# A second mixer on four parts of 128 tokens instead of two halves of 256, with its side tiles kept in SBUF and a router of one-hot products

## The chip, the cores and the metric

One core of a Trainium2 chip runs the whole program in one launch. The metric is the device time of one execution in microseconds (us). Before the change three runs took 3859.07, 3864.57 and 3869.43 us; the median is 3864.57 us. The trace is of one further execution, which took 3868.05 us.

## The reference, cut to what matters

512 tokens of 1024 columns, all in float32, go through two blocks. The first block (a mixer and product-key experts, where each token picks 128 rows out of two tables of 16384 rows) ends in a norm; the second block has two mixers side by side and 32 experts.

```python
x = x + gate1 * mix                                   # first block
h = rmsnorm(x, norm2_w[l]) * (1.0 + scale2) + shift2
x = x + gate2 * peer(h, ...)                          # per token: 128 rows of u, 128 rows of v
...
u, v = expert_u[idx], expert_v[idx]
act = gelu(einsum('td,thkd->thk', xb, u))             # "dots"
return einsum('thk,thkd->td', gate * act, v)          # "sums"
...
p = rmsnorm_2(x, attn_norm_g) @ w_in                  # second block: 10528 columns
y_a = rwkv7_mix(p[rwkv])      # a recurrence over the tokens, here in chunks of 64
y_b = ssd_mix(p[z, xbc, dt])  # a convolution of 4 taps, a recurrence in chunks of 128, gated by silu(z)
x = x + (g_a * (y_a @ w_up_rwkv) + g_b * (y_b @ w_up_ssd)) @ w_out
x = x + hier_moe(h)           # top group, top 2 of its 8 experts; 1024 assignments
out = rmsnorm(x, final_norm_g)
```

Both recurrences and the convolution run forward over the tokens, so a later part of the tokens needs only a small state of the earlier one. Every token meets all the weights of the second block: w_in with 43 MB, the three matrices behind it with 17 MB.

## The kernel before

Activations lie transposed in SBUF, features on partitions and tokens along the row (`xT`, `hT`: 8 tiles of 128 x 512). The mixers work on halves of 256 tokens (`Half`, L54). Weights come from HBM through four slots in `m.weights`, each a load of 1 MB (8 x 128 rows x 256 columns, rows of 1 KB); `project` (L284) fills a slot when its tiles have been multiplied, and `prefetch` (L272) fills all four ahead of time.

The work of `Peer` (L1211) is the product-key experts. GpSimd gathers 128 rows of 4 KB at a time (0.5 MB, L1268) into a ring of 12 slots; a "step" uses one slot: a dot (L1343) or a weighted sum (L1349) on VectorE, or, for the sums of tokens 0 to 127, a diagonal matrix made on VectorE (L1337) and two products on TensorE (L1361). There are 128 steps for each of four tiles of 128 tokens and each of two tables, 1024 in all. `sequence` (L1236) fixes their order. The steps stand in VectorE's queue in between the work of the mixers: after each piece of mixer work `beside(m, dve, us)` tells how long the engine would otherwise be free, and `go` (L1314) puts one step for each `pace` (1.8, 1.1 or 1.45) of it. The order is thus fixed when the program is built, and the engines wait for one another by semaphores alone. Each block of work ends in `meet`, where four engines wait for one another.

The stages, in order:

1. The first block's mixer, query projection and picking for tokens 0 to 255.
2. The same for tokens 256 to 511, with steps in between. The picks of this half are made at the end (`key_scores`), while TensorE does the diagonal sums of tile 0.
3. `peer.finish(1)` (L1377): the steps left of tiles 0 and 1, and nothing else. The sums of tile 1 are 128 steps in a row.
4. `after_first` and `second_mixer` for tokens 0 to 255, with the 512 steps of tiles 2 and 3 in between; `peer.finish(2)` ends them.
5. `after_first` and `second_mixer` for tokens 256 to 511, with nothing beside it.
6. `second_experts`: a norm, the rows turned back, `route`, `slot_columns`, 16 pairs of experts (L2775, 12 MB of weights each, in a ring of four buffers of 4 MB), `combine`.

`second_mixer` itself is: a norm; `project` of 26 tiles of w_in (r, k, v and the small ranks; ScalarE shifts each tile, L1995 to L1997, and VectorE keeps it, L2001); `rwkv` up to the chunks; `rwkv_chunks` (L1796) with one turn for each 64 tokens; the rest of `rwkv`; `ssd`; a norm; `second_merge` with three projections of 8 tiles. The other 56 tiles of w_in (16 z, 24 x, 16 gates) are multiplied by `Spare` (L1464) inside `rwkv_chunks`, 14 to a turn, from four slots of 0.5 MB (rows of 512 bytes), in between the small products of the recurrence, so that TensorE has work while VectorE and ScalarE answer. Each such tile is taken out of its bank by ScalarE (L1550 to L1559), an x tile is convolved by VectorE (L1536, L1539), and all go to `projected` in HBM (L1280); `second_ssd` and `second_merge` load them back.

`route` computes the experts' choice by a chain of small VectorE operations. It then scatters token numbers to `slot_token` in HBM (L2496) by eight indirect DMAs; `slot_columns` (L2615) loads and turns that list, and the experts gather their rows of `h_kept` by it. On SP's queue `route` has the store of `h_kept`, four loads of 4 MB, and eight stores of zeros into `y_rows` (L2472), and its block ends only when these have landed.

## Time and profile before

| | |
|---|---|
| median of 3 runs | 3864.57 us (3859.07 to 3869.43) |
| the profiled execution | 3868.05 us; span 3866.0 us, mean granted clock 0.829 |
| TensorE (PE), its weight loads (PEld) | 2701.5 us (70%), 1970.6 us (51%) |
| VectorE (DVE) | 2223.4 us (58%) |
| ScalarE (ACT), GpSimd (POOL) | 537.4 us (14%), 1331.2 us (34%) |
| DMA | 1006.32 MB, mean 260 GB/s; gathers 549.54 MB, 38.6% of 16 engines' span; loads of SP 406.66 MB, 29.2% |

The profile's slices show the stages. In the slices 10 to 23 of 40 (about 970 to 2320 us) the DMA row has 8 or 9 tenths; in the slices 24 to 32 (about 2320 to 3190 us) it has 1 to 4 tenths, and the PE row 5 to 9; in the slices 34 to 38 it has 9 tenths at 428 GB/s. The chain of waits that the page gives covers only the last stage here, so the stages are read from the windows view: for each stretch it has the busy time of each engine with its instructions, the granted clock, the busy share of the 16 DMA engines and the rate. GpSimd's busy time there is the writing of the gathers' descriptors. An instruction for two operands in float32 shows as two MATMUL records.

### The profile page before, as it was taken

How to read it: one execution, taken by the hardware profiler on the slowest of the kernel's cores; microseconds unless marked ns; L12 is line 12 of the kernel's file. 1: busy time of each engine (PE TensorE's matmuls, PEld its weight loads, DVE VectorE, ACT ScalarE, POOL GpSimd, SP SyncE). 2: the span in 40 equal slices, each digit the busy share in tenths (PEclk: the TensorE clock that was granted, in tenths of full speed). 3: DMA queues.
4: the chain of work that ended last, by engine and by line, in shares of the span. 5: the costliest groups of instructions: out<-in, count | busy, mean ns of one | idle time of the engine just before them, and what ended most of it. 6: DMA issues, size and time to landing. Idle time of an engine off the chain costs nothing. (4 is left out here: it accounts for less than half of the span.)

```text
span 3866.0 us, 44669 instructions
## 1 busy us (share of the span) xinstructions
PE 2701.5 (70%) x17677; PEld 1970.6 (51%) x17677; DVE 2223.4 (58%) x4122; ACT 537.4 (14%) x1041; POOL 1331.2 (34%) x1088
## 2 busy tenths in 40 slices
PE   5877443767970175899965473879998777587774
PEld 4756442554420164778754452758887656322221
DVE  6543898887859878778888888252222633100001
ACT  1120002100000012222211100132222210000001
POOL 0000367675777666567655455000000000100000
PEclk7988776788985597989976786979999788799997
DMA  7611689897999997899988798413332233899996
GB/s 275 205 44 55 224 297 339 275 373 288 360 350 372 361 342 261 277 339 362 368 303 272 238 356 292 136 43 95 98 102 64 77 131 110 335 427 428 428 428 283
DMA packets 446736, 1006.32 MB, mean 260 GB/s; under 512 B 30525, under 2 KB 292039, under 8 KB 431175
## 3 DMA queue, kind: packets, MB, share of 16 engines
q0 software_dynamic: 151200, 549.54, 38.6%
q1 hardware_dynamic: 262948, 406.66, 29.2%
q10 hardware_dynamic: 32387, 47.38, 3.4%
q8 instruction: 133, 2.18, 0.2%
q14 instruction: 68, 0.56, 0.0%
HBM read 972.01 MB, written 31.47 MB: 260 GB/s over the span
## 5 line engine op out<-in xcount | busy, mean ns | idle before, releaser
L1268 POOL DMA_INDIRECT ring<-in_peer_u_dram,index x512 | 696.8, 1361 | 760.9 <-POOLq L190 418.8
L1268 POOL DMA_INDIRECT ring<-in_peer_v_dram,index x512 | 597.6, 1167 | 337.7 <-DVE h_rows_b L1349 163.9
L334 PE MATMUL bank<-hT,weights 128*128 128x256 f32 x2240 | 513.2, 393 | 179.8 <-DMA weights<-in_w_in_dram 87.9
L334 PEld LDWEIGHTS bank<-hT,weights 128*128 128x128 f32 x2240 | 441.5, 198 | 250.9 <-issue 104.1
L1513 PE MATMUL bank<-hT,weights 128*128 128x256 f32 x1792 | 426.2, 393 | 53.7 <-DVEq L149 25.9
L1513 PEld LDWEIGHTS bank<-hT,weights 128*128 128x128 f32 x1792 | 340.3, 194 | 106.2 <-issue 55.4
L1349 DVE SCALAR_TENSOR_TENSOR h_rows_b<-ring,coef,h_rows_b 128x1024 f32<-128x1024 f32 x254 | 325.6, 1282 | 37.0 <-DMA ring<-in_peer_v_dram,index 9.9
L1343 DVE SCALAR_TENSOR_TENSOR ring<-ring,h_rows_a 128x1024 f32<-128x1024 f32 x256 | 304.8, 1220 | 62.9 <-DMA ring<-in_peer_u_dram,index 60.6
L1343 DVE SCALAR_TENSOR_TENSOR ring<-ring,h_rows_b 128x1024 f32<-128x1024 f32 x256 | 299.3, 1220 | 13.0 <-DMA ring<-in_peer_u_dram,index 7.7
L2480 POOL MEMSET weights<- 128x1024 f32 x1 | 1.0, 957 | 871.3 <-POOLq L160 871.3
L2696 PE MATMUL bank<-xp_ring,weights 128*64 128x512 f32 x1024 | 252.3, 650 | 67.2 <-DMA xp_ring<-in_w_exp_gate_dram 48.7
L1361 PE MATMUL bank<-ring,weights 128*128 128x512 f32 x512 | 225.6, 602 | 9.6 <-DVE weights L1337 9.5
L2696 PEld LDWEIGHTS bank<-xp_ring,weights 128*64 128x64 f32 x1024 | 80.3, 149 | 227.4 <-issue 184.5
L2756 DVE COPY weights<-bank 128x512 f32<-128x512 f32 x16 | 11.1, 692 | 310.9 <-PE bank L2708 310.9
L1349 DVE SCALAR_TENSOR_TENSOR h_rows_a<-ring,coef,h_rows_a 128x1024 f32<-128x1024 f32 x127 | 163.1, 1284 | 14.0 <-DVE h_rows_a L1349 1.0
L1361 PEld LDWEIGHTS bank<-ring,weights 128*128 128x128 f32 x512 | 98.5, 194 | 136.0 <-issue 136.0
L2800 POOL DMA_INDIRECT weights<-h_kept,mo_columns x16 | 15.1, 941 | 384.3 <-PE bank L2682 365.6
L2721 PE MATMUL bank<-xp_ring,weights 128*64 128x512 f32 x512 | 115.0, 601 | 23.8 <-DMA xp_ring<-in_w_exp_down_dram 23.1
L1854 DVE TENSOR_TENSOR rc_Y<-rc_Y,bank 128x512 f32<-128x512 f32 x40 | 27.3, 683 | 181.2 <-PE bank L1822 181.2
L334 PE MATMUL bank<-ssd_y,weights 128*128 128x256 f32 x512 | 116.6, 392 | 19.7 <-DVEq L149 8.9
L977 PE MATMUL bank<-ident,h_rows_a 128*128 128x128 f32 x16 | 3.7, 424 | 181.1 <-ACTq L142 181.1
L334 PEld LDWEIGHTS bank<-ssd_y,weights 128*128 128x128 f32 x512 | 100.6, 197 | 36.4 <-issue 21.9
(513 smaller groups left out, 3959.8 us busy)
## 6 DMA issues: line engine op xcount, KB each, us to landing
xp_ring<-in_w_exp_gate_dram SPq DMA_DIRECT2D x16, 4096.0 KB, 35.7
xp_ring<-in_w_exp_up_dram SPq DMA_DIRECT2D x16, 4096.0 KB, 33.4
xp_ring<-in_w_exp_down_dram SPq DMA_DIRECT2D x16, 4096.0 KB, 34.4
weights<-in_w_in_dram SPq DMA_DIRECT2D x112, 512.0 KB, 4.0
weights<-in_w_in_dram SPq DMA_DIRECT2D x54, 1024.0 KB, 10.8
weights<-in_w_out_dram SPq DMA_DIRECT2D x16, 1024.0 KB, 13.1
weights<-in_peer_w_query_dram SPq DMA_DIRECT2D x16, 1024.0 KB, 7.9
weights<-in_w_up_ssd_dram SPq DMA_DIRECT2D x16, 1024.0 KB, 11.7
```

The lines of the kernel that those rows point to most:

```text
L334: ins = pe.matmul(m.ps[b][:, 0:TH], m.weights[:, s, k, c * P:(c + 1) * P], rhs(k), start=(k == 0), stop=(k == k_tiles - 1))
L977: ins = pe.transpose(m.ps[k][:, t * P:(t + 1) * P], src[:, t, k * P:(k + 1) * P], m.ident[:, :])
L1268: pool.indirect_dma_start(out=self.ring[:, n % RING, :], out_offset=None, in_=self.tables[table], in_offset=bass.IndirectOffsetOnAxis(ap=s ...
L1343: dve.scalar_tensor_tensor(out=slot, in0=slot, scalar=1.0, in1=row, op0=ALU.mult, op1=ALU.mult, accum_out=dots[:, j:j + 1]).then_inc(self. ...
L1349: dve.scalar_tensor_tensor(out=row, in0=slot, scalar=coef[:, j:j + 1], in1=row, op0=ALU.mult, op1=ALU.add).then_inc(self.free, 1)
L1361: ins = pe.matmul(bank[:, :], self.diag[:, j % self.DIAGS, :], self.ring[:, n % RING, h * 512:(h + 1) * 512], start=(j == 0), stop=(j == P ...
L1513: ins = pe.matmul(self.m.ps[3 + q % 2][:, 0:TH], self.weights[:, (q + 2) % self.SLOTS, k, :], self.half.h[:, k, :], start=(k == 0), stop=( ...
L1854: dve.tensor_tensor(dst[:, :, :], dst[:, :, :], bank3(5 + j), ALU.add).then_inc(xy_kept, 1)
L2696: ins = pe.matmul(m.ps[2 + j][q, :], self.xT[:, k, q], self.ring[:, slots[j], h, k * DE:(k + 1) * DE], start=(k == 0), stop=(k == KT - 1))
L2721: ins = pe.matmul(m.ps[5 + b][q, :], self.hidT[:, k, q], self.ring[:, slot, h, k * D + b * 512:k * D + b * 512 + 512], start=(k == 0), sto ...
L2756: dve.tensor_copy(self.hidT[:, :, :].rearrange("p k r -> p (k r)"), self.m.ps[4][:, :]).then_inc(self.h_kept, 1)
L2800: pool.indirect_dma_start(out=x.xr[:, p % 2, :], out_offset=None, in_=x.h_rows, in_offset=bass.IndirectOffsetOnAxis(ap=columns[:, p:p + 1] ...
```

## The change

Tokens are taken through the second mixer in four parts of 128 (`Part`), each part begun once `peer.finish` has the sums of its own tile of rows. Tile 3 is the last of the steps' order, tile 2 now comes whole before it. The three first parts stand in the stretch with steps; the fourth comes behind it.

- `project`, `norm`, `group_norm` and `rwkv` work on 128 columns instead of 256, and `beside` in `project` is halved with them. `rwkv_chunks` has two turns in each part instead of four, with 28 side tiles in a turn instead of 14.
- The side tiles (z, x, gates) are written where they are used, in SBUF; nothing goes to `projected`. Their order is `xxzxxzxxzzgggg` twice, and there are four row buffers for the convolution instead of two.
- `ssd` runs once for each part. Its state goes to HBM at the end of a part (1 MB, on SP's queue) and comes back at the start of `ssd` of the next.
- Of `second_experts`, the rows are turned back inside `route`, behind the router's products, and kept by ScalarE; the eight stores of zeros now stand in `after_first` of the last part; the counts above 64, 128, ... are one comparison and one sum; the three counting products are over all tiles at once; `slot_token` is gone: for each of 8 columns of assignments VectorE writes a one-hot of the place in the slot (128 wide) and one of the block times the token (24 wide), and TensorE multiplies them into the list.
- `combine` takes the root and scales tile by tile.

```diff
+class Part:
+    def __init__(self, m, j):
+        self.j, self.first, self.last = j, j == 0, j == T // TQ - 1
+        tokens = slice(j * TQ, (j + 1) * TQ)
+        self.x, self.h = m.xT[:, :, tokens], m.hT[:, :, tokens]
+        self.room = m.halves[1 - j * TQ // TH].h
@@ project
-                beside(m, dve, 0.44 * k_tiles)
+                beside(m, dve, 0.44 * k_tiles * width / TH)
@@ Peer.sequence
         steps += second_dots[at:] + all_of(1, 1)
-        for table in range(2):
-            for tile in range(HT, TT):
-                steps += all_of(tile, table)
+        for tile in range(HT, TT):
+            steps += all_of(tile, 0) + all_of(tile, 1)
@@ Peer.finish
-        m, end = self.m, halves * self.HALF_STEPS
+        m, end = self.m, self.plan.index((tile, 1, PICKS - 1)) + 1
+        self.pace = LATE_PACE
@@ Spare
-    KINDS = "zxgxzxgxzxgxzg"
+    ROWS = 4
+    KINDS = "xxzxxzxxzzgggg" * 2
...
-        act.dma_start(self.dest[self.FIRST[kind] + n], y).then_inc(self.stored[q % self.SLOTS], 16)
@@ rwkv_chunks, TensorE
-                    i = spare.multiply(pe, i, 2 * KT)
+                    i = spare.multiply(pe, i, (4 * PER_STEP - 2) * KT)
...
-                        i = spare.multiply(pe, i, KT // 2 if l <= 2 else KT)
+                        i = spare.multiply(pe, i, PER_STEP * (KT // 2 if l <= 2 else KT))
@@ ssd
+            @block.sync
+            def _(sp):
+                if not part.first:
+                    sp.dma_start(state, carry.ssd).then_inc(carry.ssd_landed, 16)
@@ second_ssd
-                for j in range(SG):
-                    sp.dma_start(z[:, 4 * j:4 * j + 4, :],
-                                 projected[4 * j:4 * j + 4].rearrange("k p t -> p k t")).then_inc(z_landed[j], 16)
+            if not part.last:
+                sp.dma_start(carry.ssd, state).then_inc(carry.ssd_stored, 16)
             prefetch(m, sp, *then)
@@ route
-                        pool.indirect_dma_start(
-                            out=slot_token.rearrange("b (s a) -> (b s) a", a=1),
-                            out_offset=bass.IndirectOffsetOnAxis(ap=dest[:, n:n + 1], axis=0),
-                            in_=token[:, t:t + 1], in_offset=None).then_inc(scattered, 16)
+                for n in range(TT * TOP):
+                    dve.tensor_scalar(hot_slot[:, n, :], slots[:, :], placef[:, 0, n:n + 1], None,
+                                      ALU.is_equal).then_inc(spread, 1)
+                    dve.tensor_scalar(hot_block[:, n, :], blocks[:, :], placef[:, 1, n:n + 1],
+                                      token[:, n // TOP:n // TOP + 1], ALU.is_equal, ALU.mult).then_inc(spread, 1)
...
+                for n in range(TT * TOP):
+                    pe.wait_ge(spread, 2 * n + 2)
+                    ins = pe.matmul(m.ps[3][:, 0:BLOCKS], hot_slot[:, n, :], hot_block[:, n, :],
+                                    start=(n == 0), stop=(n == TT * TOP - 1))
@@ two_blocks
-                    peer.finish(1)
                     early.close()
-                    with stage(m):
-                        after_first(m, first, rows[0], cols1, at1, (w_in_2[0], R_TILES))
-                    rows_a.close()
-                    second_mixer(first, second, rk_masks, own, ssd_small)
-                    peer.finish(2)
+                    for part in m.parts[:-1]:
+                        peer.finish(part.j)
+                        with stage(m):
+                            after_first(m, part, rows[part.j // HT][:, part.j % HT:part.j % HT + 1], cols1, at1, (w_in_2[0], R_TILES))
+                        if part.j == HT - 1:
+                            rows_a.close()
+                        second_mixer(part, rk_masks, own, ssd_small)
+                    peer.finish(TT - 1)
                     m.stretch, m.side = None, None
```

Three places show what moves. The first is VectorE behind the picks. `ring` and `h_rows` are the gathered rows and the rows that they are dotted with or summed into; `weights<-ident,coef` is a diagonal; `xT<-bank,mod,xT` opens `after_first`. Before, the sums of tile 1 stand ahead of it:

```order
L1337 TENSOR_SCALAR weights<-ident,coef 128x128 x8
L147 UNCONDITIONAL_BRANCH
L1380 UNCONDITIONAL_BRANCH
L1333 TENSOR_TENSOR coef<-coef,gate 128x128
L1346 TENSOR_SCALAR h_rows_a<-ring,coef 128x1024
L1349 SCALAR_TENSOR_TENSOR h_rows_a<-ring,coef,h_rows_a 128x1024 x127
L147 UNCONDITIONAL_BRANCH
L1393 UNCONDITIONAL_BRANCH
L1371 COPY h_rows_a<-bank 128x512 x2
L147 UNCONDITIONAL_BRANCH
L980 UNCONDITIONAL_BRANCH
L985 SCALAR_TENSOR_TENSOR xT<-bank,mod,xT 128x256 x8
```

Now:

```order
L1356 TENSOR_SCALAR weights<-ident,coef 128x128 x8
L161 UNCONDITIONAL_BRANCH
L1411 UNCONDITIONAL_BRANCH
L1390 COPY h_rows_a<-bank 128x512 x2
L161 UNCONDITIONAL_BRANCH
L998 UNCONDITIONAL_BRANCH
L1003 SCALAR_TENSOR_TENSOR xT<-bank,mod,xT 128x128 x8
L1352 TENSOR_TENSOR coef<-coef,gate 128x128
L1365 TENSOR_SCALAR h_rows_a<-ring,coef 128x1024
L1368 SCALAR_TENSOR_TENSOR h_rows_a<-ring,coef,h_rows_a 128x1024 x2
```

The second mixer's work begins 128 steps earlier, and the sums of tile 1 stand within it.

The second place is VectorE inside a turn of `rwkv_chunks`, in the stretch with steps. `rc_Y` and `rc_X` (in `weights` now) are the matrices of the recurrence; `spare_leaving` and `x_tiles` are convolved side tiles. Before:

```order
L1854 TENSOR_TENSOR rc_Y<-rc_Y,bank 128x512
L1854 TENSOR_TENSOR rc_X<-rc_X,bank 128x512
L1536 TENSOR_SCALAR spare_leaving<-spare_rows,cols 128x256
L1539 SCALAR_TENSOR_TENSOR spare_leaving<-spare_rows,cols,spare_leaving 128x256 x3
L1343 SCALAR_TENSOR_TENSOR ring,dots<-ring,h_rows_b 128x1024 x8
```

Now:

```order
L1880 TENSOR_TENSOR weights<-weights,bank 128x512 x2
L1571 TENSOR_SCALAR x_tiles<-spare_rows,cols 128x128
L1574 SCALAR_TENSOR_TENSOR x_tiles<-spare_rows,cols,x_tiles 128x128 x3
L1571 TENSOR_SCALAR x_tiles<-spare_rows,cols 128x128
L1574 SCALAR_TENSOR_TENSOR x_tiles<-spare_rows,cols,x_tiles 128x128 x3
L1368 SCALAR_TENSOR_TENSOR h_rows_a<-ring,coef,h_rows_a 128x1024 x8
```

A level of the recurrence keeps its 8 steps and has two convolved tiles of half the width instead of one.

The third place is SP's queue over one part, the second of the four. It is the same for all parts but for the state, which the first does not load and the last does not store. `L286` is `prefetch`, with 16 loads of 1 MB behind the chunks; `L321` stands for the nine further loads of `project`; `L1543` are the 56 side tiles:

```order
L286 DMA weights<-in_w_in_dram 128x8x256 x4
...
L321 DMA weights<-in_w_in_dram 128x8x256
...
L1543 DMA weights<-in_w_in_dram 128x8x128 x2
...
L1543 DMA weights<-in_w_in_dram 128x8x128 x54
...
L1771 DMA rk_gates<-in_rwkv_w_g_dram 128x1024
...
L2125 DMA sd_state<-ssd_state 128x2048
...
L286 DMA weights<-in_w_up_rwkv_dram 128x8x256 x4
...
L2356 DMA ssd_state<-sd_state 128x2048
L286 DMA weights<-in_w_up_ssd_dram 128x8x256 x4
...
L286 DMA weights<-in_w_up_ssd_dram 128x8x256 x4
...
L286 DMA weights<-in_w_out_dram 128x8x256 x4
```

Before, the same loads of weights stand twice in the program, for 256 tokens each; now they stand four times.

## Rows read from the trace of the kernel before

**Rows 1.** Windows view: PE, PEld, DVE, ACT, POOL busy, granted clock, DMA share, GB/s.

```profile
1142.00:1319.00 177.00, 0.00 (x0) 0.00 (x0) 162.58 (x128) 0.00 (x0) 138.02 (x127) 0.50 0.98 369
1319.00:2411.00 1092.00, 766.35 (x6366) 626.61 (x6366) 893.71 (x1313) 194.14 (x412) 668.32 (x502) 0.81 0.89 312
```

**Rows 2.** Windows view, stages of the first 256 tokens, beside the expert rows.

```profile
1319.00:1364.00 45.00, 14.92 (x48) 11.90 (x48) 33.74 (x62) 7.24 (x19) 19.84 (x17) 0.65 0.86 300
1364.00:1482.00 118.00, 98.61 (x416) 83.75 (x416) 83.76 (x154) 18.70 (x78) 80.76 (x62) 0.93 0.98 357
1482.00:1557.00 75.00, 31.24 (x96) 18.49 (x96) 67.95 (x106) 22.47 (x35) 45.73 (x29) 0.57 0.65 210
1557.00:1991.00 434.00, 390.05 (x4760) 334.17 (x4760) 356.56 (x543) 107.41 (x211) 291.38 (x216) 0.93 0.95 337
1991.00:2255.00 264.00, 147.56 (x677) 105.90 (x678) 218.00 (x311) 38.31 (x69) 133.08 (x99) 0.68 0.79 269
2255.00:2359.00 104.00, 83.97 (x371) 72.41 (x369) 87.83 (x105) 0.00 (x0) 68.31 (x55) 0.92 0.98 357
```

**Rows 3.** Windows view, the same stages of the other 256 tokens, alone.

```profile
2421.00:2445.00 24.00, 11.24 (x32) 8.64 (x32) 10.54 (x20) 5.47 (x17) 0.00 (x0) 0.78 0.31 98
2445.00:2540.00 95.00, 92.95 (x416) 81.05 (x416) 13.07 (x28) 18.69 (x78) 0.00 (x0) 0.97 0.35 105
2540.00:2600.00 60.00, 38.84 (x130) 24.87 (x130) 38.63 (x53) 22.15 (x35) 0.00 (x0) 0.66 0.17 44
2600.00:2971.00 371.00, 363.50 (x4728) 312.11 (x4727) 102.37 (x176) 99.94 (x181) 0.00 (x0) 1.00 0.34 93
2971.00:3150.00 179.00, 130.26 (x726) 94.70 (x726) 99.85 (x214) 38.84 (x69) 0.00 (x0) 0.77 0.25 82
3150.00:3240.00 90.00, 85.63 (x384) 74.17 (x384) 19.90 (x49) 0.00 (x0) 0.00 (x0) 0.97 0.36 117
2421.00:3240.00 819.00, 722.43 (x6414) 595.53 (x6414) 284.37 (x538) 185.09 (x380) 0.00 (x0) 0.91 0.31 91
```

**Rows 4.** DMA view of 1557 to 1991: queues, then issues with landing.

```profile
q0 software_dynamic: 30112, 109.67, 65.8%
q1 hardware_dynamic: 59376, 28.45, 23.6%
...
weights<-in_w_in_dram SPq DMA_DIRECT2D x54, 512.0 KB, 11.3
```

**Rows 5.** DMA view of 1364 to 1482: the same.

```profile
q0 software_dynamic: 8791, 32.03, 72.1%
q1 hardware_dynamic: 9360, 9.44, 23.6%
...
weights<-in_w_in_dram SPq DMA_DIRECT2D x9, 1024.0 KB, 27.4
```

**Rows 6.** Costliest groups on the page: VectorE's steps for the expert rows.

```profile
L1349 DVE SCALAR_TENSOR_TENSOR h_rows_b<-ring,coef,h_rows_b 128x1024 f32<-128x1024 f32 x254 | 325.6, 1282 | 37.0 <-DMA ring<-in_peer_v_dram,index 9.9
...
L1343 DVE SCALAR_TENSOR_TENSOR ring<-ring,h_rows_b 128x1024 f32<-128x1024 f32 x256 | 299.3, 1220 | 13.0 <-DMA ring<-in_peer_u_dram,index 7.7
```

**Rows 7.** Timeline of the router: start, duration, engine, line.

```profile
3261.54 6.51 PE L948 MATMUL bank<-ident,hT 128*128 128x128 f32 x32 [10.52 <-PEq L160]
...
3294.03 0.29 DVE L2581 COPY mo_rank<-bank 128x128 f32<-128x128 f32 x1 [6.34 <-PE bank L2516]
...
3303.03 0.17 DVE L2608 TENSOR_TENSOR mo_dest<-mo_base,mo_rk 128x8 uint32<-128x8 f32 x1
...
3329.32 0.37 SPq L2625 DMA_DIRECT2D slot_rows<-slot_token  x1
...
3331.33 0.18 DVE L2636 CAST mo_columns<-bank 128x24 uint32<-128x24 f32 x1 [20.86 <-issue]
```

**Rows 8.** Windows view, the router, the experts, the last stage.

```profile
3340.00:3833.00 493.00, 393.85 (x1720) 143.80 (x1718) 32.41 (x47) 37.11 (x63) 12.32 (x14) 0.93 0.96 407
3833.00:3866.00 33.00, 0.00 (x0) 0.00 (x0) 15.26 (x14) 6.18 (x10) 8.06 (x8) 0.50 0.55 207
```

682 lines of the change are left out of this document (340 added, 342 removed).

## The prediction

> **What bounds the kernel now.** I read the slices first, then the windows view cut at the stages, then the DMA view of two stages. The point from which the kernels differ is where TensorE's diagonal sums of tile 0 end and VectorE is left with the sums of tile 1 alone (1142 us). From there the kernel before has three stretches until the experts' norm at 3240 us, 2098 us in all. (a) 1142 to 1319: 128 steps with no mixer work; PE is at 0, the DMA engines at 0.98 [rows 1]. (b) 1319 to 2421: the mixer of 256 tokens with 512 steps beside it, and the end of the steps. To the last step at 2411 the DMA share is 0.89, PE is busy 766 of 1092 us, VectorE 894 [rows 1]. By stage the two widest, `project` and the chunks, stand at 0.98 and 0.95 of the DMA engines, while `rwkv` ahead of the chunks and the stages behind them are at 0.65 and 0.79, with VectorE 68 of 75 and 218 of 264 us busy [rows 2]. (c) 2421 to 3240: the other 256 tokens alone, 819 us, PE busy 722, DMA at 0.31; in the chunks PE has 363.5 of 371 us [rows 3]. So the stretch with steps is bound by the DMA engines with VectorE close behind, and the tail by TensorE.
>
> **The change, part by part.** Prices of transfers: a gather costs 0.658 x 434 / (109.67 / 0.524) = 1.365 us of all 16 engines in the chunks [rows 4] and 0.721 x 118 / 61.1 = 1.39 us in `project` [rows 5]; I take 1.39. A 1 MB load costs 0.236 x 118 / 9 = 3.09 us [rows 5], a side tile of 0.5 MB 0.236 x 434 / 54.3 = 1.89 us [rows 4]. One pass over the second mixer's weights is 13 + 16 such loads and 56 side tiles: 90 + 106 = 196 us, with some 9 for the small matrices and the 2 MB of state: 205 us of all DMA engines. It does not shrink with the tokens. Before, two passes (and some 43 us a pass to store and load `projected`, of which about half falls in the chunks); now four.
>
> The steps of each part, counted from VectorE's order: 275 in part 0, 266 in part 1, 99 in part 2 (the last in its first turn of chunks), none in part 3. They are the 640 that were left at 1142 us, and the gathers themselves cost what they did. The finishes between the parts are left with none. DMA work of part 0: 275 x 1.39 + 205 = 587 us; of part 1: 266 x 1.39 + 205 = 575.
>
> Part 0 by stages, each the largest of its demands. (A) the two norms, 17 steps: 36 us (before 45 [rows 2]). (B) `project`, 31 steps: 31 x 1.39 + 9 x 3.09 = 71 us of DMA, against 47 us of PE (half of 93 [rows 3]): 72. (C) `rwkv`, 25 steps: VectorE, with 25 x 1.25 us [rows 6] and some 23 of its own (38.6 for 256 columns [rows 3]): 57. (D) two turns of chunks, 54 steps each: 54 x 1.365 + 28 x 1.89 = 127 us of DMA a turn, where before a turn had 108.5 (434 / 4 [rows 2]) at 14 side tiles; at the 0.97 of such stages 130, so 260. PE needs only 92 of the 130 (371 / 4 [rows 3]), VectorE 54 x 1.25 + some 30. (E) from the chunks to `second_merge`, 69 steps: VectorE 69 x 1.25 + 52 (half of 100 [rows 3] and a little) = 138, at its former share of 218 / 264: 165. (F) the merge, 25 steps: 35 + 8 x 3.09 = 60: 62. Sum 652 us. Part 1 in the same way, with 16, 32, 25, 108, 56 and 29 steps: 35 + 73 + 57 + 260 + 150 + 65 = 640. Together 1292 us for 1162 of DMA work, a share of 0.90; the stretch before had 0.89, so the sum asks no more of the engines than they gave.
>
> Part 2 has steps in A, B, C and half of its first turn: 35 + 73 + 57, then a turn with 26 steps, 36 + 53 = 89 us of DMA below the 92 of PE, where I take 100; a turn alone 98; E alone 100; F alone 45: 508 us. Part 3, alone: 15 + 4 (the zeros, 4 MB on the queue with the prefetch), 49, 31, 196, 100, 45 = 440. The alone figures are half of those in rows 3 (24, 95, 60, 371, 179, 90) and what does not halve: the product and the spacing do, since two passes of 128 columns cost what one of 256 does, but each x tile's four convolution steps and ScalarE's three to four small instructions are now paid per 128 columns, and `rwkv`, `ssd` and the norms start their chains four times. That is 3 us in C, 6 in a turn, 10 in E. The bound on these from below is 0 (they hide beside PE as they do now, 363.5 of 371 busy [rows 3]) and from above twice as much: 0 to 75 us over both parts, I take 43. In a turn ScalarE also loads its tables less often, since the kinds come in groups; it is no bound at 100 of 371 us [rows 3], so I count that at nothing.
>
> Sum to 3240's counterpart: 1292 + 508 + 440 = 2240, against 2098: **142 us longer**. In words: PE no longer stands idle in (a), and the tail shrinks from 819 to about 440 and some of part 2; but two passes, 410 us of DMA work, are added for the 86 of `projected` that go, and most of it where the DMA engines were already the bound.
>
> **The router and the end.** The block of `route` lasted until 3329.3, though the places were ready at 3303.2 [rows 7]: scatter, zeros and the store are behind it, then the list comes back from HBM and the experts' products begin at 3340. Now behind the places stand some 20 small VectorE operations at about 0.15 us, eight short products, and ScalarE's copies of the turned rows, some 9 us; the list needs no trip. That is 19 us less than from 3303 to 3331.5. The turn ahead of the router leaves the path: 6.51 us of PE [rows 7] and a copy and a barrier, 8 us. In front of the rank (VectorE waits 6.34 us for the counting products [rows 7]) 5 us go, since the products go from 14 to three, and TensorE's turn of the rows lies there behind the router's choice. Together 32 us, and since the experts are bound by DMA (0.96 at 407 GB/s [rows 8]) and their first 16.8 MB were landed anyway, all 32 move the end; bounds 15 (the 2 MB store waits behind the experts' 16.8 MB, and the block ends on it) to 40. `combine`: three of four scalings and stores leave the tail of a 33 us stage [rows 8]: 3 us. Together 35 us.
>
> **Sum.** 3868 + 142 - 35 = 3975 us against the profiled execution, which lies 3.5 us above the median of the runs shown: about **3972 us**.
>
> On the size of rows. The side tiles' packets are 512 bytes, and a side tile costs 1.89 us [rows 4], which is 278 GB/s. The Trainium skill (DMA: Bandwidth & Descriptors, Specifications) puts the least transfer for line rate at 512 bytes, so that these should run like any other; the experts' stretch moves 407 GB/s [rows 8], by which a tile would cost 1.29 us, a pass 34 us less, and the two and a half passes beside the steps some 85 us less (about 3887). The trace disagrees, and the sum goes by the trace.
>
> **Rivals.**
> 1. The ring covers what the stages leave open, so the change is faster. Where VectorE is the bound (C, E), gathers can run 12 slots ahead, 17 us of DMA work each time, and the change has twice as many such seams. For it: landing of a gather is not what VectorE waits on (37.0 us in 254 sums [rows 6]). Against: the same ring gave 0.89. At a share of 1.0 parts 0 and 1 take 1162, part 2 some 475 and part 3 409: 2046, less by 52 than before, and with the 35 it ends at 3778. It decides from 2133 us on (2098 and the 35): that is a share of 0.98 in parts 0 and 1 if the rest is as I have it, or 0.93 if parts 2 and 3 also reach those figures.
> 2. TensorE's clock. In the tail it is granted 0.97 and 1.00 in `project` and chunks, in the stretch 0.93, but 0.57 and 0.68 where PE works less than 60% of the time [rows 2, 3]. Now B and D ask 47 of 72 and 92 of 130 us of it, shares of 0.65 and 0.71, where before they had 0.84 and 0.90. If the clock granted there is some 0.75, between its levels of 1.2 and 2.4 GHz, a turn's 92 us become 115 to 120; with waits for weights (a 1 MB load lands after 27.4 us, a side tile after 11.3 [rows 4, 5]) they are no longer hidden: some 15 us a turn and 5 a `project`, for five turns and three projects 90 us: 4060.
> 3. The parts cost in tokens what the halves did (DMA has room, the mixer's work just slides into (a)): before, (b) has 0.11 x 1092 = 120 us of free DMA engines. If the added pass in the stretch used them fully, 120 of the 142 go: 3852, no change to measure. Against it: that free time lies in C and E, where SP's loads have nothing to fetch.
>
> **Chances.** The forecast 0.60 (own range 3920 to 4020), rival 2 0.22, rival 1 0.10, rival 3 with the faster packets 0.08, of which a part lies within 0.3%. About 0.3% is what a measurement of this kernel tells from no change. Slower 0.85, same 0.04, faster 0.11. The range reaches from 3870, which leaves out rival 1, to 4070, which takes in rival 2: 8 in 10.
>
> **What would show it.** Right: the first transposes of the second mixer at about 1142 us; no long row of sums alone; a turn of chunks in parts 0 and 1 of 125 to 135 us with the DMA share above 0.93, in part 3 of 92 to 102 with PE above 0.9; the last gather near 2650 us (1142 + 1292 + 165 + 50) instead of 2411; DMA bytes up by two passes of 61 MB less the 29 of `projected`, with 6 of state to about 1105 MB; the experts' first product some 68 us behind the end of the merge, where it was 100. Wrong: turns in parts 0 and 1 near 110 us (rival 3, or side tiles below 1.5 us each); a granted clock below 0.8 in B and D with the DMA share under 0.9 (rival 2); a part 3 above 470, then the small instructions cost more than their upper bound; experts that begin only when the store of the rows has landed.

## The result and the profile after

The changed kernel takes 4108.9 us (median of four runs, 4094.9 to 4116.5), the kernel before 3867.0; the ratio is 1.062, 95% interval 1.059 to 1.066. It is slower by 242 us, where 107 were forecast. Its profiled execution took 4116.5 us with a span of 4114.7. One execution each of two later kernels, the end alone and the freed banks, ran slow (5799 and 4668 us); medians and ratios leave them out.

Cut at the same stages as before, in us (forecast, then measured; A and F, the two norms and the merge, together, since the turn of the rows lies on their border):

| | A + F | B project | C rwkv | D chunks | E rest | sum |
|---|---|---|---|---|---|---|
| part 0 | 98, 105 | 72, 78 | 57, 62 | 260, 274 | 165, 158 | 652, 677 |
| part 1 | 100, 109 | 73, 80 | 57, 62 | 260, 268 | 150, 140 | 640, 659 |
| part 2 | 80, 91 | 73, 80 | 57, 62 | 198, 225 | 100, 102 | 508, 560 |
| part 3 | 64, 70 | 49, 50 | 31, 38 | 196, 219 | 100, 100 | 440, 477 |

Together 2373 us where 2240 were forecast and 2098 stood before: 275 us longer. Of the 133 us above the forecast 72 lie in D, 33 in A and F, 21 in B, 22 in C, and E is 15 below. From the end of the merge to the experts' first product it is 79 us (before 100.5), the experts take 493.5 (before 493.3), the last stage is 2 us shorter: 24 us back of the 35 forecast.

First the windows view of the changed kernel, stages B to F of part 0 (PE, PEld, VectorE, ScalarE and GpSimd busy, granted clock, DMA share, GB/s):

```profile
1167.00:1245.00 78.00, 59.53 (x416) 58.41 (x416) 45.92 (x58) 15.93 (x78) 37.92 (x32) 0.80 0.98 342
1245.00:1307.00 62.00, 18.77 (x96) 14.00 (x96) 54.40 (x80) 16.68 (x35) 34.96 (x25) 0.50 0.70 230
1307.00:1581.00 274.00, 214.15 (x2841) 200.70 (x2841) 192.37 (x298) 46.44 (x158) 138.10 (x109) 0.88 0.90 296
1581.00:1739.00 158.00, 75.06 (x432) 58.12 (x432) 128.97 (x274) 25.55 (x53) 96.36 (x66) 0.64 0.90 312
1739.00:1817.00 78.00, 51.09 (x392) 50.12 (x392) 47.68 (x91) 1.59 (x2) 38.22 (x32) 0.83 0.98 346
```

These answer to [rows 2]. In B and F the DMA engines are the bound as before (0.98), in C VectorE with 54 of 62 us. D is the new thing: the DMA share is 0.90, lower than the 0.95 of the same stage before, though there is more to move. (In part 1 it is 0.95 over 268 us.)

The same view: from the start of part 0 to the last expert row, part 2's chunks, then part 3 alone (D, E), the experts and the last stage:

```profile
1140.00:2713.00 1573.00, 993.62 (x9946) 909.87 (x9948) 1155.46 (x1902) 273.91 (x869) 821.95 (x626) 0.78 0.90 305
2645.00:2870.00 225.00, 199.47 (x2841) 188.45 (x2842) 94.19 (x162) 46.43 (x158) 17.29 (x15) 0.95 0.58 166
3145.00:3364.00 219.00, 194.25 (x2811) 183.24 (x2810) 61.17 (x135) 46.48 (x158) 0.00 (x0) 0.95 0.48 126
3364.00:3464.00 100.00, 67.55 (x496) 54.90 (x496) 54.54 (x142) 25.14 (x53) 0.00 (x0) 0.79 0.31 101
3590.00:4084.00 494.00, 396.35 (x1720) 144.94 (x1720) 32.87 (x49) 37.84 (x64) 13.04 (x14) 0.93 0.96 406
4084.00:4115.00 31.00, 0.00 (x0) 0.00 (x0) 15.62 (x16) 6.95 (x13) 8.09 (x8) 0.50 0.58 221
```

The stretch with steps has the share that the forecast used, 0.90. But compare D alone, 3145 to 3364, with [rows 3]: 219 us against half of 371, and PE, which worked 363.5 of 371 us there, now works 194 of 219. In part 2 only the first turn has steps, and its chunks take 225. The last rows answer to [rows 8].

The DMA view of part 0's chunks (queues: packets, MB, share; issues: count, KB, us to landing) answers to [rows 4]:

```profile
q0 software_dynamic: 14316, 52.14, 50.4%
q1 hardware_dynamic: 59107, 28.45, 39.3%
...
weights<-in_w_in_dram SPq DMA_DIRECT2D x54, 512.0 KB, 9.7
```

A side tile costs 0.393 x 274 / 54.3 = 1.98 us of the DMA engines (1.89 before); a gather 0.504 x 274 / (52.14 / 0.524) = 1.39 (1.365). On the page, the bytes and the gathers, and PE's 3584 side products with what they waited for:

```profile
DMA packets 594585, 1105.49 MB, mean 269 GB/s; under 512 B 30909, under 2 KB 438819, under 8 KB 578211
...
L1286 POOL DMA_INDIRECT ring<-in_peer_u_dram,index x512 | 692.4, 1352 | 824.5 <-POOLq L204 412.4
...
L1553 PE MATMUL bank<-hT,weights 128*128 128x128 f32 x3584 | 495.4, 303 | 219.1 <-DMA weights<-in_w_in_dram 63.4
```

The bytes are those of the forecast, 1105 MB. The last line says what it had not in it: PE's side products were held up 219 us in all, and only 63 of that was for weights. The waits view of PE, over the whole span, has the rest (engine, line, waited for: us in total, times, longest):

```profile
PE bank L1553 <- DMA weights<-in_w_in_dram: 63.4, 23, 6.8
PE bank L1553 <- DVEq L163: 62.0, 3, 21.2
...
PE bank L1553 <- ACT spare_rows L1587: 39.0, 22, 3.0
...
PE bank L1553 <- ACT z_tiles L1589: 25.7, 14, 3.3
...
PE bank L1553 <- ACT g_tiles L1591: 20.9, 12, 2.4
```

62 us (and 8 more in part 3) are the ends of the blocks ahead of the chunks, and the weights are waited for in parts 0 and 1 alone (30.4 and 33.1 us). The last three lines, 85.6 us, are waits for ScalarE. So the trace was asked for PE's waits in part 3's chunks, where no expert row is gathered or summed:

```profile
PE bank L1553 <- ACT spare_rows L1587: 10.3, 6, 3.0
PE bank L1553 <- ACT g_tiles L1591: 7.0, 4, 2.4
PE bank L1553 <- ACT z_tiles L1589: 6.3, 4, 2.4
```

These 23.6 us, all of PE's waits there, ended on ScalarE emptying one of the two PSUM banks of the side tiles. The timeline of ScalarE in one such place (start, duration):

```profile
3178.30 0.31 ACT L1599 ACTIVATE x_tiles<-x_tiles 128x128 f32<-128x128 f32 x1 [7.52 <-DVE x_tiles L1574]
...
3178.66 0.27 ACT L1587 COPY spare_rows<-bank 128x128 f32<-128x128 f32 x1
3178.81 0.29 ACT L1589 ACTIVATE z_tiles<-bank 128x128 f32<-128x128 f32 x1
...
3185.33 1.28 ACT L1591 ACT_TABLE_LOAD   x1
...
3195.83 0.59 ACT L1918 COPY weights<-bank 128x512 f32<-128x512 f32 x1 [7.70 <-PE bank L1848]
```

It waited 7.52 us for VectorE's convolution of an x tile while the bank of the next stood full (PE waits 2.94 us there, to 3179.07), and at 3195.83 it copies PE's next step of the chunk first, though both banks are full and wait for it.

And the router, on the timeline, answering to [rows 7]: the store of the rows is issued, the list of rows per block is ready, the first gather starts, the first product of the experts:

```profile
3554.26 0.40 ACTq L3023 DMA_DIRECT2D h_kept<-weights  x1
...
3563.88 0.18 DVE L2636 CAST mo_columns<-bank 128x24 uint32<-128x24 f32 x1 [0.30 <-PE bank L2535]
...
3582.88 0.96 POOL L2811 DMA_INDIRECT weights<-h_kept,mo_columns  x1 [46.90 <-POOLq L2486]
...
3590.49 1.98 PE L2707 MATMUL bank<-xp_ring,weights 128*64 128x512 f32 x4 [0.83 <-issue]
```

From the list to the gather there are 19 us: the block ends only when the 2 MB store has landed. The DMA view of that stretch has its landing, 27.5 us:

```profile
h_kept<-weights ACTq DMA_DIRECT2D x1, 2048.0 KB, 27.5
```

### The profile page after: what moved, and what is told of

The parts are those of the page before. It is cut to its first block and busy times, and to the rows that moved or that the text cites. A ratio compares the mean times of both kernels' runs of the same rounds, so it can differ in the third digit from the quotient of the medians.

```text
span 4114.7 us, 55012 instructions
## 1 busy us (share of the span) xinstructions
PE 2831.7 (69%) x21898; PEld 2233.2 (54%) x21898; DVE 2307.5 (56%) x4758; ACT 607.9 (15%) x1642; POOL 1342.3 (33%) x1082
## 5 line engine op out<-in xcount | busy, mean ns | idle before, releaser
L1286 POOL DMA_INDIRECT ring<-in_peer_v_dram,index x512 | 620.9, 1213 | 550.8 <-DVE h_rows_b L1368 233.4
L349 PE MATMUL bank<-hT,weights 128*128 128x128 f32 (+1 forms) x3072 | 541.8, 343 | 232.7 <-DMA weights<-in_w_in_dram 131.3
L1553 PE MATMUL bank<-hT,weights 128*128 128x128 f32 x3584 | 495.4, 303 | 219.1 <-DMA weights<-in_w_in_dram 63.4
L349 PEld LDWEIGHTS bank<-hT,weights 128*128 128x128 f32 x3072 | 493.2, 208 | 281.0 <-issue 150.1
L1553 PEld LDWEIGHTS bank<-hT,weights 128*128 128x128 f32 x3584 | 471.8, 216 | 233.6 <-issue 161.1
L1880 DVE TENSOR_TENSOR weights<-weights,bank 128x512 f32<-128x512 f32 x72 | 49.1, 686 | 248.0 <-PE bank L1848 248.0
L349 PE MATMUL bank<-x_tiles,weights 128*128 128x128 f32 x1024 | 126.9, 290 | 36.0 <-ACTq L156 15.8
L349 PEld LDWEIGHTS bank<-x_tiles,weights 128*128 128x128 f32 x1024 | 125.1, 205 | 37.9 <-issue 30.2
L2029 DVE SCALAR_TENSOR_TENSOR proj_rk<-bank,rk_keep_mu,rk_earlier 128x128 f32<-128x128 f32 x104 | 36.2, 348 | 136.2 <-ACT rk_earlier L2025 136.2
```

Of the source, the lines that this page charges most:

```text
L349: ins = pe.matmul(m.ps[b][:, 0:width], m.weights[:, s, k, c * P:(c + 1) * P], rhs(k), start=(k == 0), stop=(k == k_tiles - 1))
L1286: pool.indirect_dma_start(out=self.ring[:, n % RING, :], out_offset=None, in_=self.tables[table], in_offset=bass.IndirectOffsetOnAxis(ap=s ...
L1553: ins = pe.matmul(self.m.ps[3 + q % 2][:, 0:TQ], self.weights[:, (q + 2) % self.SLOTS, k, :], self.part.h[:, k, :], start=(k == 0), stop=( ...
L1880: dve.tensor_tensor(dst[:, :, :], dst[:, :, :], bank3(5 + j), ALU.add).then_inc(xy_kept, 1)
L2029: return dve.scalar_tensor_tensor(out=p[:, t, :], in0=bank[:, 0:TQ], scalar=keep_mu[:, t:t + 1], in1=earlier[:, t % LATE, 0:TQ], op0=ALU.m ...
```

## The experiments

The twelve runs stand in three sessions of four: the kernel before took 3865 us in the first, 3944 in the second and 3935 in the third. In the later two the chunks of a half beside gathers are 45 to 65 us longer in the traces with the mixer of before, those of a part of the changed kernel 10 to 19, and the chunks alone are the same to 2 us. So times are compared within a session only.

**The end alone, on the mixer of before.** Taken from the changed kernel: the norm, the turn, `zeros`, the router, `combine`, `second_experts`; two lines in the main function:

```diff
-                after_first(m, second, rows_b, cols1, at1, (w_in_2[0], R_TILES))
+                after_first(m, second, rows_b, cols1, at1, (w_in_2[0], R_TILES), zeros(m, tmp, y_rows[PAIRS * P:, :]))
```

> The kernel before with only the changed kernel's end: the router by one-hot products, the norm without the turn and the barrier, the zeros stored ahead, combine tile by tile. The mixer stays on two halves of 256 tokens. Theory: the experts are bound by their weights, whose first 16.8 MB land during the router, so what the router loses moves the end one for one: from the end of the merge to the experts' first product 78 us as in the changed kernel (before 100), combine 2 to 4 us shorter, together 3835 to 3850 us (ratio 0.992 to 0.996). Rival: the weights' DMA decides when the experts are done, whenever the first product begins; then the experts' stretch grows by what the router loses and the time stays within 5 us of the kernel before.

Ratio 0.9949 (0.9929 to 0.9968), some 20 us faster; the first product 79.6 us behind the merge, the experts 494 us. The theory holds; what the router loses moves the end. It also shows that the end is no part of the loss.

**Without the bytes of two passes.** One load of three as an example; it is the same in `prefetch` and in `Spare.load`, and set for parts 1 and 3:

```diff
+                if m.sliver:
+                    sp.dma_start(m.weights[0:16, s, 0:1, :],
+                                 wv[0:16, 0:1, bass.ds((i * SLOTS + s) * SLOT_COLS + col0, SLOT_COLS)]).then_inc(m.w_landed[s], 16)
+                    return
```

> The changed kernel, but parts 1 and 3 load only a sliver of each weight tile (16 partitions, one k tile) and multiply what lies there; all steps and instructions stay. It leaves the bytes of two of the four passes out. Theory (the DMA engines are the bound of parts 0 and 1, with PE and VectorE some 100 us behind): part 1 has 599 - 206 = 393 us of DMA work left and is then bound by VectorE (483 us busy of 659) and by the turn of about 109 us that PE needs alone; it falls from 659 to 530 to 560 us, a turn from 134 to 110 to 115. Part 3, whose weights land unseen, stays within 6 us of 476. Rival (VectorE, PE and ScalarE hold each other up in the order of their programs and DMA is only filled around that): part 1 stays above 620 us.

Part 1 took 583 us instead of 659, part 3 471 instead of 477, in the one execution that there is. The windows view of this kernel, part 1 and its chunks:

```profile
1817.00:2400.00 583.00, 400.50 (x4273) 367.86 (x4273) 481.69 (x827) 111.27 (x346) 350.69 (x266) 0.81 0.75 252
1957.00:2188.00 231.00, 203.82 (x2840) 192.79 (x2840) 189.00 (x314) 46.37 (x158) 133.10 (x104) 0.93 0.70 236
```

The share fell from 0.91 to 0.75, some 162 us of DMA work (206 were counted for a pass), and that gave 76 us. The forecast of 530 to 560 was too bold, the rival of above 620 is out: the DMA engines are the bound, and others stand close behind. Over the part VectorE has 482 of 583 us. In the chunks (115.5 us a turn, forecast 110 to 115) it is PE: it works 204 of 231 us at a granted clock of 0.93 and waits 25.4 for ScalarE's banks, 229 together. (The numbers of this run's router are others, so its total says nothing.)

**Side tiles in large packets.**

```diff
-        sp.dma_start(self.weights[:, (q + 2) % self.SLOTS], self.w[:, :, c0:c0 + P]).then_inc(self.landed[q % self.SLOTS], 16)
+        sp.dma_start(self.weights[:, (q + 2) % self.SLOTS].rearrange("p k c -> p (k c)"), self.w[:, q % KT, n * P:n * P + KT * P]).then_inc(self.landed[q % self.SLOTS], 16)
```

> The changed kernel, but each side tile of 512 KB is read from whole rows of the matrix (128 packets of 4096 bytes instead of 1024 of 512 bytes), the same bytes from another place, so the products get other numbers. Theory (the size of the packets sets the price): a tile costs 1.55 to 1.65 us of the 16 DMA engines instead of 1.94, 56 tiles a part: some 20 us less DMA work in each of parts 0 and 1 and 12 in part 2, nothing in part 3, together 40 to 50 us less: about 4062 us. Rival (512 bytes run at the full rate and the tiles are dear because they share with the gathers): the price stays above 1.85 us and the time within 10 us of 4109.

4051.5 us (two runs), 57 less than the changed kernel. The DMA view of part 0's chunks in this kernel, and the windows of the chunks of parts 0 and 1:

```profile
q0 software_dynamic: 14519, 52.84, 56.8%
q1 hardware_dynamic: 10657, 28.45, 32.3%
...
weights<-in_w_in_dram SPq DMA_DIRECT2D x54, 512.0 KB, 7.5
```

```profile
1315.00:1554.00 239.00, 203.99 (x2840) 192.54 (x2840) 192.28 (x298) 46.43 (x158) 139.98 (x110) 0.92 0.90 342
1959.00:2187.00 228.00, 200.68 (x2840) 189.66 (x2840) 188.57 (x314) 46.44 (x158) 138.65 (x103) 0.94 0.94 360
```

A tile costs 0.323 x 239 / 54.3 = 1.42 us instead of 1.98, and these chunks fall from 274 and 268 to 239 and 228 us; those of part 3 stay (220). The price goes with the packets; that the bytes also lie elsewhere was not tried apart. The gain is larger than the theory's 40 to 50 us. PE's waits show how: it waited 30.4 and 33.1 us for weights in these chunks of the changed kernel and not at all here, where a tile lands after 7.5 us instead of 9.7, and its own work falls from 214 and 215 us to 204 and 201 at a higher granted clock. The waits for ScalarE's banks stay, 27.7 and 25.4 us.

**ScalarE: the bank freed sooner, the Silu later.** The lag of `leave`, and in `take`, where the wait for the bank also moves behind the first small copy:

```diff
+LAG = 8
...
-                    if q >= 2:
-                        spare.leave(act, q - 2)
+                    if q >= LAG:
+                        spare.leave(act, q - LAG)
...
-            act.copy(self.halo[:, (self.part.j + 1) % 2, n, :], bank[:, TQ - self.TAPS + 1:])
             act.copy(u[:, self.TAPS - 1:], bank).then_inc(self.taken, 1)
+            act.wait_ge(self.taken, q + 1)
+            act.copy(self.halo[:, (self.part.j + 1) % 2, n, :], u[:, TQ:TQ + self.TAPS - 1])
```

> The changed kernel with ScalarE's work on side tiles in another order: the Silu of a convolved tile comes 8 tiles later instead of 2, and the small copies of the three carried columns stand outside the time in which the bank is held. Theory (with 128 columns a side tile takes PE 1.9 us, and PE waits for ScalarE, which holds the bank while it waits up to 7.5 us for VectorE's convolution): PE's waits for banks in a turn alone, 12 us, fall below 5, a turn alone from 109 to 100 to 104; part 3 from 476 to 460 to 466, part 2 10 us less, parts 0 and 1 unchanged because they are bound by DMA: 4080 to 4090 us. Rival (what makes a turn longer than half of the former two is the start of each product of 128 columns): less than 5 us.

4106.7 us (three runs): no change. D of part 3 went from 219 to 209 us, but E from 100 to 105. PE's waits in part 3's chunks, of this kernel:

```profile
PE bank L1556 <- ACT g_tiles L1596: 12.3, 6, 2.4
PE bank L1556 <- ACT spare_rows L1590: 4.1, 4, 1.0
PE bank L1556 <- ACT z_tiles L1594: 1.9, 2, 0.9
```

Still 18 us. The Silus now fall between the gates' Sigmoids, so ScalarE loads its tables, 1.28 us each, 23 times in these chunks instead of 8 (the waits on `g_tiles` rose from 7.0 to 12.3 us), and about 1 us a seam was left: ScalarE's copy of PE's step comes before both full banks. By its own criterion the rival had won; the waits said rather that the wrong part of the order was changed.

**The store together with the second half of the weights**, on the kernel with the end alone:

```diff
                 for p in range(2):
+                    if p:
+                        sp.wait_ge(rows_kept, 2 * TT)
                     for j in range(2):
```

> The kernel before with the changed end, and one thing more: of the experts' first four weight loads (4 MB each) the last two are issued only when the rows to be stored are ready, together with the store of 2 MB. Theory: in the changed kernel the gather of the first rows waits 19 us behind the list, because the store, issued at 3554.3, lands at 3581.8 behind the 16.8 MB of weights; the DMA engines then stand still for some 17 us. Now the store lands some 10 us after it is issued, the first product follows the end of the merge by 60 to 66 us instead of 79, and the end comes 10 to 15 us earlier: 3835 to 3842 us. Rival: the later half of the weights lands that much later, so the experts wait for weights and the end stays at 3850.

Ratio 0.9953 (0.9930 to 0.9977), as without; the first product 78.9 us behind the merge. The DMA view of its router:

```profile
h_kept<-weights ACTq DMA_DIRECT2D x1, 2048.0 KB, 28.7
```

The theory fell: the store needs 28.7 us even when it starts together with the loads. The DMA view of a stretch in which both are under way, 3361 to 3381, shows how they share (q10 is the store, q1 the loads):

```profile
q1 hardware_dynamic: 431, 6.80, 79.8%
q10 hardware_dynamic: 432, 1.77, 21.5%
```

The engines take one 4 KB packet of the store for one 16 KB packet of the loads. At 4 KB of every 20, and 428 GB/s in all, 2.1 MB need 25 us. The same stretch of the changed kernel (3558 to 3576) has 390 and 392 packets.

**ScalarE's order at the seams**, on the changed kernel:

```diff
-    KINDS = "xxzxxzxxzzgggg" * 2
+    KINDS = "xxxxxxzzzzgggg" * 2
...
-                ends = [3 * PER_STEP, 4 * PER_STEP + 1] + [2 * PER_STEP * (l + 1) for l in range(2, R_LEVELS)]
+                ends = [8, 11, 14, 18, 22, 26]
...
+                    for q in range(q0, q0 + 2):
+                        pass_on(q)
                     for n, dst in enumerate((VT, BT, KT_)):
```

and the copies as in the try with the freed banks, with a lag of 4. The work is the same, but `KINDS` orders it for all engines: SP's loads, PE's products and VectorE's convolutions of the side tiles come in the new order too.

> The changed kernel with ScalarE's program in another order, all work the same: it empties the two banks of side tiles before it waits for PE's next step of the chunk (before, it left two full until it had copied that step), copies the carried columns outside the time in which a bank is held, and the kinds come as six x, four z, four gates, with the Silu of an x tile 4 tiles later, so that ScalarE loads its tables as rarely as before. Theory (the excess of a turn alone, 109 against a half of two former turns, 92, is for 10 us PE's waits for a bank at seven seams a turn, for 6 us the start of 128-column products): PE's waits in part 3's turns fall from 23.6 to below 8 us, D of part 3 from 218 to 200 to 204, part 2 about the same 15 us, parts 0 and 1 by 0 to 10 because DMA bounds them; 4065 to 4085 us. Rival (the seams are PE's own start, and ScalarE's order only moves waits, as in the last attempt): within 8 us of 4109.

4080.7 us with 3944 before (ratio 1.035); the changed kernel itself did not run beside it, so the measure is the later one below. That the time lies within the expected 4065 to 4085 is luck: these were meant against 3865 before. D of part 3 took 184 us, less than the 200 to 204 expected and about half of the 371 of before [rows 3].

**Side tiles in pairs**, on the end with the store:

```diff
-        sp.dma_start(self.weights[:, (q + 2) % self.SLOTS], self.w[:, :, c0:c0 + P]).then_inc(self.landed[q % self.SLOTS], 16)
+        sp.dma_start(self.pairs[:, (q // 2 + 1) % 2], self.w[:, :, c0:c0 + 2 * P]).then_inc(self.landed[q // 2 % 2], 16)
```

> The same as the kernel before with the changed end and the early store, and the side tiles loaded in pairs of one kind (256 columns, packets of 1024 bytes, 1 MB a load, kinds zzxxggxxzzxxgg). Theory: a tile costs 1.55 us of the DMA engines instead of 1.85 to 1.9; 56 of them stand beside the gathers, so the chunks of the first 256 tokens fall from 434 to about 415 us, the others stay at 369: 15 to 20 us less than without pairs, 3818 to 3826. Rival: a pair is fetched only when both tiles of the pair before last are done, so PE waits for it; the chunks of the first half stay at 434 or grow, those of the second grow.

Ratio 0.9963 (0.9942 to 0.9984), no gain: D of the first half 496 us with pairs, 497 without, though the DMA work of its side tiles fell by some 15 us (0.207 of 497 us to 0.177 of 496).

**All of it on the changed kernel.**

> The changed kernel with all that is known to help: ScalarE's order as in the seams kernel, side tiles in pairs, the store before the second half of the experts' first weights. Theory (two passes more are what the change costs, and only their price per byte can be lowered): 22 us of DMA work less in each of parts 0 and 1, half of that in part 2, 13 us at the end, with the seams' 30: about 4015 us (4000 to 4040), still some 150 above the kernel before. Rival: with 128 columns a pair lasts PE only 3.9 us, and it waits for each: above 4060.

4117 us, above the 4081 of the seams alone in the same session: the rival. D of part 3 took 192 us instead of 184. With two slots of a pair each, a load can start only when two tiles are done, and cheaper bytes are of no use if they are asked for later: that fits both misses and the gain of the large-packet run, which kept four slots, but no run takes the slots apart from the rest.

**The changed kernel as a measure, and the seams with a better end.** The seams kernel, and in place of the wait above `sp.wait_ge(h_stored, 16)`.

> The changed kernel once more, as the measure for the next two on the same chip, since the chip of the last four ran the kernel before at 3944 us instead of 3865, all of the difference in the stages with gathers. Expected ratio to the kernel before as first measured, 1.059 to 1.066; if the other chip's slowness is in the gathers alone, 1.05 to 1.06 on a slow one.

4166.4 us, ratio 1.0607 (1.0583 to 1.0631).

> The changed kernel with ScalarE's program in the order of the seams kernel, and at the end the last two of the experts' first four weight loads held back until the 2 MB of rows are stored. Theory: part 3's chunks 184 us as in the last call (218 in the changed kernel), part 2's 203 (225), parts 0 and 1 0 to 15 us shorter, 50 to 70 us together; at the end 10 to 15 us less; so 60 to 80 us below the changed kernel of this call. Rival (the shorter turns of the last call were given back in parts 0 and 1, where DMA bounds): below 45 us.

4067.4 us, ratio 1.0352 (1.0329 to 1.0375): 99 us below, more than the 60 to 80 expected. The windows of the chunks of parts 1, 2 and 3, first of the changed kernel, then of this one:

```profile
2000.00:2287.00 287.00, 230.94 (x2840) 211.81 (x2840) 188.54 (x313) 46.37 (x158) 142.36 (x108) 0.86 0.90 299
2678.00:2913.00 235.00, 205.00 (x2840) 192.07 (x2840) 94.59 (x163) 46.36 (x158) 17.65 (x15) 0.93 0.56 160
3190.00:3407.00 217.00, 191.56 (x2797) 180.72 (x2792) 61.55 (x136) 46.39 (x158) 0.00 (x0) 0.96 0.47 126
```

```profile
1999.00:2260.00 261.00, 220.32 (x2840) 203.48 (x2840) 188.02 (x314) 51.91 (x158) 136.95 (x100) 0.88 0.94 309
2648.00:2851.00 203.00, 197.06 (x2841) 184.93 (x2842) 94.01 (x162) 51.61 (x158) 17.30 (x15) 0.96 0.65 184
3125.00:3310.00 185.00, 185.00 (x2818) 174.85 (x2817) 59.93 (x133) 50.94 (x154) 0.00 (x0) 1.00 0.57 151
```

In part 3 PE works 185 of 185 us at a granted clock of 1.00, where it had waits and 0.96; there is not one wait of PE left in that stretch. Part by part the kernel gave back 7, 24, 36 and 31 us, 97 of 98 in the chunks, and the end some 6. In the chunks of the four parts of the changed kernel PE waits 33, 31, 24 and 24 us for ScalarE's banks, here never; they became 6, 27, 32 and 32 us shorter. Beside the gathers a piece came back as waits for weights: 17.5 and 17.1 us in parts 0 and 1, where there were 2.3 and 7.0. The rival is out: part 1 kept 24 us, at a DMA share of 0.94 instead of 0.90. Which of the three edits (the order of the kinds, the order of ScalarE's copies, the lag) does it is not taken apart; the lag and the small copies alone did not, in the try with the freed banks.

**The end of before, the second half held until the store has landed.**

> The kernel before with the changed end, and the last two of the experts' first four weight loads held back until the 2 MB store has landed (in the last try they went out with it, and the store still took 28.7 us: its 4 KB packets went turn by turn with 16 KB packets of weights). Theory: the store lands within 8 us, the gather starts as soon as the list is there, the first product follows the merge by 60 to 66 us instead of 79 and the experts then have their weights as before: 10 to 15 us less than the kernel with the changed end alone, ratio 0.990 to 0.992. Rival (the experts are bound by the bytes from the first load on, and holding them back costs what it brings): ratio 0.995 as without.

Ratio 0.9931 (0.9911 to 0.9951), the lowest ratio of all versions that ran. The DMA view of its router:

```profile
h_kept<-weights ACTq DMA_DIRECT2D x1, 2048.0 KB, 10.2
weights<-h_kept,mo_columns POOLq DMA_INDIRECT x3, 11.4
```

The store lands after 10.2 us, not 28.7, as the turn by packets would have it, and the gather starts 12 us sooner (still 7 behind the list, the cause is open). But the gather now lands 11.4 us after its issue among the 16 KB packets (5.4 in the run before, where all loads had landed by then), and the first product came at 75 us instead of 79: 4 us where 13 to 19 were expected. Against the end alone (0.9949) the intervals overlap, so the gain is not shown.

**Without the bytes, with the new order.**

> The changed kernel with ScalarE's new order, and parts 1 and 3 again load only a sliver of each weight tile, which leaves the bytes of two of the four passes out. Question: what stood behind the 583 us that part 1 took without its bytes. Theory (PE's waits for ScalarE's banks were that second bound in the chunks): its chunks fall from 231 to 200 to 212 us, part 1 to 555 to 565. Rival (VectorE with its 108 steps a part of chunks is the second bound): the chunks stay above 220.

Chunks of part 1 in 249 us, in one execution (261 with all bytes in the same session, 287 in the changed kernel): above 220, so the theory is out by its own number. The windows row, and PE's waits in it (one of 21.1 us for the block to begin lies ahead and is left out):

```profile
1973.00:2223.00 250.00, 217.60 (x2840) 198.19 (x2840) 188.30 (x315) 52.13 (x158) 136.83 (x102) 0.91 0.64 212
```

```profile
PE bank L1865 <- issue: 13.4, 32, 1.6
PE bank L1862 <- DVE weights L1897: 9.0, 2, 5.4
PE bank L1568 <- issue: 4.5, 9, 0.7
```

They don't bear out the rival either. PE works 218 us, at a granted clock of 0.91, waits 9 for VectorE and none for ScalarE, and stands idle 18 in short gaps that end on nothing the profile shows: 245 of 250. VectorE is busy 188 and waits most of the rest. So PE stands behind the DMA engines in the chunks. Its work there is 218 us where the same chunks take it 185 alone at a clock of 1.00; the gaps are not in the first session's trace without the bytes (231 us), so the two sessions can't be set against each other.

## Why the prediction was wrong

The sign and its cause held: two more passes over the weights, 410 us of DMA work, for the 177 us in which PE had stood idle. The bytes came out at 1105 MB, the stretch ran at the share of 0.90 that was used, the starting point was right, there is no row of sums alone. Without ScalarE's stalls (and with 6 us less at the end) the change costs 132 us, 4067 against 3935, where the forecast said 107. A named sign of being wrong was met: part 3 took 477 us, above 470.

**The step that failed** is in the paragraph on parts 2 and 3: "In a turn ScalarE also loads its tables less often [...] it is no bound at 100 of 371 us [rows 3], so I count that at nothing", and with it that a turn alone takes 98 us. ScalarE is busy 46 of 219 us and still set the time; it does load its tables less often (8 times for 128 tokens, before 33 for 256). What counts is not its share but how long a bank stays full: at 256 columns a side tile kept PE busy 3.7 us and ScalarE's detours (a copy of 0.59, a table of 1.28, a wait for a convolution) hid behind it, all but 5.6 us in four turns; at 128 columns it is 1.9 to 2.1 us, and PE waits 23.6 us in two turns. That the width did it, and not the order of the kinds that the change brought with it, is argued: no run has one without the other. The upper bound of 75 us for both tail parts was made by doubling the small instructions' own time (twice 43 would be 86), which can't catch a wait.

In part 3 the waits are the whole miss of D, 219 us where 196 were forecast. With them gone D takes 185 us, the half of 371: the 6 us a turn that the forecast added for narrow tiles aren't there. The new order, with all work the same, took 93 us out (99 with 6 at the end), in all four parts, more than the 72 that D missed by. By the ratio of that run, 1.035, the time would stand near 4003, inside the forecast's own range; that is an estimate over two sessions.

**Mis-sized terms.** Parts 0 and 1: the gathers cost 1.44 to 1.46 us over a part instead of 1.39, a side tile in the chunks 1.98 and 1.92 instead of 1.89, a MB 3.2 and 3.15 instead of 3.09; at a share of 0.91 of 677 and 659 us that makes 616 and 600 us of DMA work instead of 587 and 575, where these parts missed by 25 and 19. B is 6 to 7 us longer, A and F together 7 to 9. In D the same trace has 20 and 18 us of waits for banks beside it, so how much of these parts is the price of transfers and how much ScalarE is not taken apart. C was 5 us too low in three parts and 7 in the last; E of parts 0 and 1 together 17 too high.

**The router.** 22 us instead of 32. The named sign was met in this form: the gather began 19 us after the list, when the store had landed. The lower bound (15) had that in it; the value chosen did not. One 4 KB packet of the store for each 16 KB packet of the loads, a fifth of the rate, is what made the store slow.

**The rivals.** Rival 1 (share 1.0) is out: 0.90 and 0.91. Rival 2 came nearest in time (4060), by luck for the larger part: the granted clock in B and D of parts 0 and 1 was 0.80 to 0.82 and 0.88 to 0.89, not 0.75, and a turn missed its forecast by most where the clock was highest, by 11 us in part 3 at 0.95, by 7 and 4 in parts 0 and 1, not by 15. What it describes is there in small: PE's work in D of parts 0 and 1 is 214 and 215 us instead of the 184 of the forecast, and with 30 and 33 us of waits for weights and 20 and 18 for banks it fills the stage. Rival 3 is out: turns of 137 and 134 us beside gathers, not 110. In the large-packet run a tile cost 1.42 us in packets of 4096 bytes, in the changed kernel 1.98 in packets of 512. By the Trainium skill (DMA: Bandwidth & Descriptors, Specifications) 512 bytes reach line rate; that run disagrees.

## What to carry to other kernels

When a tile is made narrower, don't ask whether the engine that empties its bank is busy, but whether its longest detour still fits into the time of the tiles that the banks hold; then order its program so that full banks come first. A pass over weights costs its bytes whatever the number of tokens, so an idle PE beside busy DMA engines is not free time. And a small transfer on which a stage waits should be on its way before the large ones, not among them; the runs here gained 4 us by it.

## What the hardware showed beyond that

- Two queues in flight shared the DMA engines packet for packet, 431 of 16 KB against 432 of 4 KB: so 2 MB in 4 KB packets landed 28.7 us after issue among such loads, and 10.2 us when half of these were held back.
- The same work in two sessions: 3865 and 3944 us for the kernel before, with the chunks alone at 369 us (371 in the window of [rows 3]) in the traces of both, taken with the mixer of before. The stages with gathers differ. In the slower sessions PE there has short gaps that end on nothing the profile shows (12.4 us in 34 of them before the small products of part 1's chunks, changed kernel), where the first session's trace has none. The cause is open.
- With its waits gone, PE in part 3's chunks was granted 1.00 instead of 0.96 of the full clock (2.4 GHz): of the 32 us that went there 23.6 were the waits, and most of the rest are the side products, 110.7 us before and 103.1 after.
